# Squares for nine norms made on ScalarE behind the high parts, in place of GpSimd

## The reference

```python
def rms_norm(x, g):
    xf = x.astype(jnp.float32)
    y = xf * lax.rsqrt(jnp.mean(xf * xf, axis=-1, keepdims=True) + EPS)
    return (y * g.astype(jnp.float32)).astype(x.dtype)

# first block, each layer i
h = rms_norm(x, norm_mix[i]);  ...  x = x + o @ w_out[i]
x = x + memory_cross_attention(rms_norm(x, norm_cross[i]), m, ...)
x = x + conv_gated_mlp(rms_norm(x, norm_ffn[i]), ...)
# second block: a retention layer, then a convolution layer
fx = modulate(rms_norm_2(hx, norm_ffn[i]), sh2, sc2)
hx = hx + g2 * swiglu(fx, ffn_w1[i], ffn_w3[i], ffn_w2[i])
```

## Time and profile before

| | |
|---|---|
| median of 3 runs | 1667.44 us (1662.01 to 1670.44) |
| profiled execution, its own time | 1670.68 us |
| its span | 1669.0 us |
| PE busy | 1602.2 us (96%) |
| VectorE busy | 1181.0 us (71%) |
| ScalarE busy | 796.4 us (48%) |
| GpSimd busy | 120.0 us (7%) |

### The profile page before, as it was taken

How to read it: one execution, slowest core, us unless ns; L and a number is a source line. 1 busy time by engine, 2 the same in 40 slices (tenths; PEclk the granted TensorE clock), 3 DMA queues, 4 the chain that set the end, 5 groups by cost and what they waited for, 6 DMA issues and landing times.

```text
span 1669.0 us, 36179 instructions
## 1 busy us (share of the span) xinstructions
PE 1602.2 (96%) x12312; PEld 1481.7 (89%) x12318; DVE 1181.0 (71%) x1780; ACT 796.4 (48%) x1271; POOL 120.0 (7%) x125
## 2 busy tenths in 40 slices
PE   8999899999999989999999999989999999999998
PEld 6987679999897768999989878879999989989997
DVE  5774768888898458998867454558777678677654
ACT  4555456553455546664445212224555345454533
POOL 3000111110310011110000000000000000000000
PEclk9999899999999999999999999999999999999999
DMA  8440425558775034556935553338555765545551
GB/s 332 158 149 11 154 95 170 171 176 273 251 232 187 26 118 156 178 178 251 352 101 180 165 164 114 126 124 330 176 184 181 245 209 188 178 155 185 178 187 50
DMA packets 81014, 293.59 MB, mean 176 GB/s; under 512 B 9008, under 2 KB 10544, under 8 KB 80176
## 3 DMA queue, kind: packets, MB, share of 16 engines
q1 hardware_dynamic: 78768, 283.31, 50.4%
q10 hardware_dynamic: 2176, 9.31, 1.6%
HBM read 291.53 MB, written 1.05 MB: 175 GB/s over the span
## 4 chain that ended last, share of the span: by engine, by line
PE 72%; DVE 12%; ACT 8%; issue 5%; DVEq 1%; ACTq 1%; DMA 0%; SPq 0%; POOL 0%
PE projs L1569 37%; PE accs L1569 29%; PE ob L1569 6%; ACT WH L466 4%; DVE WL L905 3%; DVE us L1233 2%; DVE cv L1242 1%; DVE cv L1240 1%; ACT AH L529 1%; PE projs L1796 1%; DVE rstd L1002 1%; ACT FH L502 1%; DVE ring L915 1%; DVE cprod L913 0%; DMA vecs<-in_vecs 0%
## 5 line engine op out<-in xcount | busy, mean ns | idle before, releaser
L466 ACT ACTIVATE WH<-ring 128x1024 fp32r (+1 forms) x436 | 460.1, 1056 | 594.2 <-PE projs L1569 298.4
L905 DVE TENSOR_TENSOR WL<-ring,WH 128x1024 fp32r<-128x1024 f32 x436 | 541.5, 1244 | 282.3 <-ACT WH L466 280.9
L1569 PE MATMUL projs<-AH,WH 128*128 128x256 f32 (+2 forms) x2304 | 582.3, 295 | 24.6 <-ACT AH L529 8.4
L1569 PE MATMUL projs<-AL,WH 128*128 128x256 f32 (+2 forms) x2304 | 561.1, 287 | 0.3
L1569 PEld LDWEIGHTS projs<-AH,WH 128*128 128x128 f32 x2304 | 433.3, 192 | 46.3 <-ACT AH L529 13.4
L1569 PEld LDWEIGHTS projs<-AL,WH 128*128 128x128 f32 x2304 | 428.3, 191 | 10.7 <-DVE AL L1019 5.0
L1569 PE MATMUL projs<-AH,WL 128*128 128x256 f32 (+2 forms) x2304 | 328.2, 285 | 0.0
L1569 PEld LDWEIGHTS projs<-AH,WL 128*128 128x128 f32 x2304 | 299.0, 189 | 3.2
L1569 PE MATMUL accs<-FH,WH 128*128 (+1 forms) x768 | 190.6, 285 | 2.0 <-ACT WH L466 2.0
L1569 PE MATMUL accs<-FL,WH 128*128 (+1 forms) x768 | 189.7, 280 | 0.0
L1569 PEld LDWEIGHTS accs<-FH,WH 128*128 128x128 f32 x768 | 144.0, 187 | 3.3 <-issue 3.3
(11 more groups left out here) (249 smaller groups left out, 1755.6 us busy)
## 6 DMA issues: line engine op xcount, KB each, us to landing
ring<-in_stream SPq DMA_DIRECT2D x532, 512.0 KB, 3.4
W1v<-in_w ACTq DMA_DIRECT2D x2, 1024.0 KB, 5.5
W1k<-in_w ACTq DMA_DIRECT2D x2, 1024.0 KB, 8.5
D<-in_decay ACTq DMA_DIRECT2D x4, 512.0 KB, 4.8
x<-in_xT SPq DMA_DIRECT2D x2, 512.0 KB, 5.2
memT<-in_memT SPq DMA_DIRECT2D x1, 1024.0 KB, 11.3
ctxT<-in_ctxT ACTq DMA_DIRECT2D x1, 1024.0 KB, 8.8
out_y<-ybuf SPq DMA_DIRECT2D x8, 128.0 KB, 2.1
```

What stands on the lines that cost most here:

```text
L466: A(WH[:, s, :], ring[:, r % RING, :], ACT.Copy).then_inc(wh_ready, 1)
L905: V.tensor_tensor(WL[:, s, :], ring[:, r % RING, :], WH[:, s, :].bitcast(F32), ALU.subtract).then_inc(consumed, 1)
L1569: return T.matmul(out, lhsT, rhs, start=start, stop=stop, skip_group_check=True)
```

## The change

GpSimd makes no squares any more: its helpers `squared` and `squares` go, and all calls of them. In `raw_root`, which runs on ScalarE at each of the nine places behind the eight high parts, eight squares of one block each now stand between the load of the table and the copy of the sums. They go to the same buffer `scr` and count the same semaphore. PE's program is as it was.

```diff
@@ raw_root (ScalarE)
                 act.preload_act_table(ACT.Sqrt)
+                for kb in range(KB):
+                    A(scr[:, kb, :], x[:, kb, :], ACT.Square).then_inc(sq_ready, 1)
                 act.wait_ge(sq_used, 8 * n["norm"] + 8)
                 A(rms[:], misc[:, 0:S], ACT.Copy).then_inc(sum_ready, 1)
@@ GpSimd's program
-            n = dict(x=0, fl=0, fh=0)
-
-            def squared(b):
-                pair = x[:, 2 * b:2 * b + 2, :]
-                G.tensor_tensor(scr[:, 2 * b:2 * b + 2, :], pair, pair, ALU.mult).then_inc(sq_ready, 2)
-
-            def squares(per):
-
-                for b in range(4):
-                    pool.wait_ge(x_ready, n["x"] + per * (b + 1))
-                    squared(b)
-                n["x"] += 4 * per
-            pool.wait_ge(in_x, 16)
-            squared(0)
-            squared(1)
-            pool.wait_ge(in_x2, 16)
-            squared(2)
-            squared(3)
+            n = dict(fh=0)
...
-                squares(1)
-                squares(1)
...
-                if i == 0:
-                    squares(1)
-                else:
-                    n["x"] += 4
...
-            n["x"] += KB
-            squares(2)
...
-            squares(2)
-            squares(2)
```

## The result

The changed kernel took 1684.55 us (median of 6 runs, 1682.17 to 1685.14); the kernel before, in the runs beside it, 1667.0 us (6 runs, 1662.0 to 1670.81). The ratio is 1.0112 with a 95% interval of 1.0093 to 1.0132: slower by 17.6 us by the medians. The forecast was 1676.4 with a range up to 1684. The direction was right; the size was nearly double, and the time lies just outside the range.

A forecast was written before the change was run, and what follows sets the result against it. PE was taken to bound the kernel, ending last. Added waits of 9.83 us less 2.28 returned by the clock gave 7.6, plus 1.4 for a new low stretch: 9.0 over the 1667.44 median, 1676.4 us, range 1669 to 1684.

The forecast's parts named there:

- where the time goes: At nine norms PE would wait for ScalarE's first four squares behind the table load, 9.83 us in sum.
- the copy's idle time: ScalarE's idle time before copying the sums, over nine places, would fall from 40.7 us to some 20.
- no drain: At the table loads, the skill's 1.38 us drain per switch, 12.4 us more in all, would not appear.
- GpSimd's squares cost PE nothing in this order: Removing 36 GpSimd products, four per place, would free VectorE's low parts but gain PE 0.
- Rival 3: Not slower: GpSimd's hold on VectorE's low parts was in PE's path, so removal gains; 1665 us, chance 0.06.
- S0: The moment at which PE reaches the first four sums of squares at each of nine places.
- Off by size, down: the squares: Four ScalarE squares behind the load would take 1.65 us, so first sums start 2.98 us after load start.
- the clock gives some back: At six places with low clock behind the first sums, half the wait returns, up to the slow excess: 2.28 us.
- one new low stretch: One of three places clear of low clock would gain a slow period behind the first sums: 1.4 us.
- Rival 1: Clock takes more: low stretches at all three clear places, longer at two others; 14.6 us, 1682, chance 0.25.
- the cover by low-clock work: At six places half-speed products already covered more of ScalarE's time, leaving added waits of 0.72 to 1.01 us.
- The base: Profiled execution of 1670.68 us stood 3.24 above the median 1667.44, so forecast 1679.7 became 1676.4.

The follow-up runs named there:

- the wait alone: Kernel before plus four unread squares on ScalarE behind the table load, with PE awaiting the fourth before the first sums: 1688.12 us, ratio 1.0127.
- the sums moved: PE's first sums put behind the low products: 1667.88 us in the changed kernel, 1668.41 us in the kernel before.
- kernel before, gap filled: Kernel before with three idle PE products ahead of the fifth high product at each place: 1661.15 us, ratio 0.9969.
- changed kernel, both gaps filled: Changed kernel with three idle PE products ahead of the fifth high product and three ahead of the first sums: 1673.51 us, ratio 1.0048.
- squares first: Changed kernel with ScalarE's eight squares ahead of the table load instead of behind it: 1663.65 us, ratio 0.9984.
- squares first, gap filled: Changed kernel with squares ahead of the table load and three idle PE products ahead of the fifth high product: 1660.21 us, ratio 0.9972.
- the longer wait: Changed kernel with PE awaiting all eight squares, instead of four, ahead of the first sums: 1700.8 us, ratio 1.0213.

## Why the prediction was right in its direction and wrong in its size

**Right: where the time goes.** PE waits for ScalarE's fourth square at nine places, behind a table load. Both ways to take that wait away remove the loss, and the wait alone, put into the kernel before, makes it. ScalarE's work as such costs nothing that can be measured; the second four squares made no wait (the second sums start right behind the low products), and the copy's idle time fell as the moved chain required:

```profile
ACT rms L537 <- PE ob L1544: 31.9, 9, 4.8
...
PE ob L1544 <- ACT scr L535: 9.0, 9, 1.3
```

It is 31.9 us, where some 20 was expected. Eight squares pass in 2.56 us, 0.32 each and not 0.41, so they fill 23.0 us of the old idle time and not 29.5; and the copy is released 14.2 us later in sum (40.7 - 23.0 + 14.2 = 31.9) instead of 9.8.

**Right: no drain.** The squares start 0.02 us or less behind the load's end (640.09 + 1.28 = 641.37, and 641.39, at place 6). The Trainium skill ("ScalarE: Activation LUTs", section "What ACT_TABLE_LOAD costs") states a drain of about 1.38 us with each switch, 12.4 us at nine places by the prediction's estimate. The trace does not agree: no such time stands at any of the nine loads, as the rows of before had said.

**Right: GpSimd's squares cost PE nothing in this order.** VectorE's low parts ran free, and the two kernels without any wait, one with the squares on GpSimd and one with them on ScalarE, take 1661.15 and 1660.21. Rival 3 falls. By the Trainium skill ("SBUF — State Buffer", section "SBUF: two separate sides"), GpSimd and a VectorE instruction with two inputs in SBUF take one pair of ports in turn. The trace agrees as to VectorE's instruction (1310 ns at most with GpSimd at work, 486 without). The low parts' delay is hidden behind S0 in this order, and it showed in PE's rows only with the sums moved.

**Off by size, down: the squares.** S0 came 2.68 us behind the load, not 2.98: four squares end 1.34 us after they start, where I took 1.65 from four each of which waits for PE to free its buffer. The trace of the kernel before also had four that wait for nothing:

```profile
30.77 1.32 ACT L512 ACTIVATE scr<-memT 128x256 f32<-128x256 f32 x4
```

Against the rows of before the added waits sum to 7.2 us (the table's spacings), not 9.83.

**The step that failed: "the clock gives some back".** I had 2.28 us of the waits returned at the six low places, and one new low stretch of 1.4: together -0.9. Between S0 and the end of the last WL product, the measured difference is 14.4 - 7.2 = +7.2 us. The premise was that a low stretch ends at the same moment whatever PE does. The runs show that it does not. The wait is itself idle time of PE, and the low stretch goes on over it or comes behind it. At place 1 the stretch's clock went from 0.76 to 0.63, at place 4 from 0.88 to 0.63, at place 8 from 0.88 to 0.76. At places 3 and 5 it stayed at 0.88, yet they took 1.5 and 1.4 us more for 0.42 us more spacing, since the low stretch no longer lay on the high products but on the work behind the wait. Only place 2 behaved as forecast (0.76 in both, 0.18 us more). Rival 1 had placed the danger wrongly: the three places that were clear stayed clear in the profiled execution (6, 7, 9), and what the clock added was at five of those that had a low stretch already.

The same loss, taken apart by the runs: with a full clock the step from no wait (kernel before, gap filled, 1661.15) to wait (changed kernel, both gaps filled, 1673.51) is 12.4 us, which is nine times 2.68 - 1.31 = 1.37. So a full-clock wait counts at all nine places, also at those where the profile of before seemed to cover part of it: that cover was the clock's own loss, and it was not a credit. The same error is thus in the waits themselves (0.72, 0.93 and 1.01 at the six low places) and in the half of them taken back. On top the clock costs 11.0 us in the changed kernel (1684.55 - 1673.51) and 5.7 in the one before (1666.86 - 1661.15), 5.3 more. 12.4 + 5.3 = 17.7, against 17.6 measured. This takes the filled kernels as free of the clock's loss; place 1 (0.88 in both) is not quite.

In the prediction's terms, from 9.0 us: the squares were 2.6 us too dear (9.83 against 7.2), the cover by low-clock work took off 5.2 us that were paid (7.2 against 12.4), the give-back 2.3 more, and the new low stretches were put at 1.4 where 5.3 came. 9.0 - 2.6 + 5.2 + 2.3 + 3.9 = 17.8. The first error was luck: it went the other way and hid part of the rest. With the squares priced right the forecast would have been some 6.4 us.

The price of the waits does not rest on the idle products alone. Every run has its own mean granted clock, and runs with the same one can be compared: at 0.992 the kernel before takes 1661.65 us (median of 11 runs) and the changed kernel with both gaps filled 1674.2 (2 runs); at 0.984 the kernel before takes 1670.5 (8 runs) and the changed kernel 1682.2 (1 run). The waits cost 12.6 and 11.7 us by this. At 0.992 the kernels without a wait agree within 0.4 us: 1661.5 (kernel before, gap filled, 3 runs), 1661.9 (squares first, 3 runs) and 1661.7 (squares first, gap filled, 1 run).

**The base.** The profile of before was of an execution 3.7 us above the median of 1667.0, and more of it ran at the low clock than usual (mean 0.985, where runs at the median show 0.987). I moved the sum to the median by subtraction, but worked out the waits from that execution's rows, in which six of nine places were low. In a run with fewer of them the added wait is longer. That is a part of the same error.

**Open.** Why the changed kernel keeps the full clock at places 6, 7 and 9 of its profile, with 1.3 us of idle PE, and lost it there with the longer wait. And how the 5.3 us divide between places from run to run: each kernel was profiled once.

## What to carry to other kernels

Look at what stands in front of work that another engine waits for: eight squares moved ahead of a table load of 1.28 us, with no other change, took back 20.9 us, the whole loss of 17.6 and a little of the clock's. When work at the low clock seems to cover part of an added wait, price the wait as if the clock were full, and add to it, since the wait itself makes for more low clock; a factor of 1.4 to 1.5 on the full-clock wait was found here (17.6 for 12.4, 16.3 for 11.0). Where a short wait of PE can't be removed, idle products in it are worth a try: they gave 5.7 us in the kernel before (one gap) and 11.0 in the changed one (two gaps). And a profile's row must be like the case at hand: the squares' time was read off rows that waited for PE, while rows without a wait stood in the same trace.

## What the runs showed of the hardware

Squares of 128x256 whose inputs are ready follow one another on ScalarE every 0.31 us, although each one lasts 0.400 us: they overlap. PE's low stretches in this kernel respond to three idle products, 0.2 us each at the full clock, in gaps of 0.7 to 1.3 us; in the changed kernel filling one of the two gaps brings two thirds of the gain, and only the profile with both filled has a full clock at places 2 to 9. A low part that needs 474 ns on VectorE took up to 1310 with GpSimd's squares beside it, and this showed in no time that was measured, as long as PE had the first sums to do ahead of the low products.
